# First units of GLU, up and embed in another order: two first contraction halves, then both second halves

## Chip, core and metric

The kernel runs on one core of a Trainium2 chip. The metric is the device time of one execution in microseconds (us), lower being better. Three runs of the kernel before took 1865.04, 1866.92 and 1867.5 us; their median is 1866.92 us.

## What is computed

Two layers over a sequence of 512 positions of 1024 channels, each with a mixer, a gated feed-forward part with a small convolution, and a per-layer embedding. The mixer of layer 0 is a bidirectional SSD, that of layer 1 an S5 state model whose output goes through a GLU.

```
h = x
for i in range(2):
    u = rmsnorm(h, mix_norm_w[i])
    h = h + (ssd_mixer if i == 0 else s5_mixer)(u, ...)
    h = h + conv_ffn(rmsnorm(h, ffn_norm_w[i]), w_up[i], conv_w[i], conv_b[i], w_down[i])
    h = h + (p[i] @ w_proj[i]) * sigmoid(rmsnorm(h, ple_norm_w[i]) @ w_gate[i])
return rmsnorm(h, final_norm_w)
# s5_mixer ends with:  g = gelu(y);  v = g @ w_glu + b_glu;  return v[:, :1024] * sigmoid(v[:, 1024:])
# rmsnorm(x, w) = x * rsqrt(mean(x * x) + 1e-6) * w
```

All is float32.

## The kernel before

**Layout and precision.** Everything stands transposed: 128 channels on the partitions, 512 positions in the free dimension, so `h` is 8 tiles of 128x512. Each large product is made of three fp32r products: the activation is split into a rounded part (`uh`, `gh`, `gh5`, `yh`) and a residual (`ul`, `gl`, `gl5`, `yl`), and so is the weight (`w_hi`, `w_lo`).

**Units.** Weights come in units of 128x1024: four contraction tiles by 256 output channels. SyncE loads a unit into one of two `w_raw` buffers, ScalarE rounds it to `w_hi` (`hi`, L848), VectorE subtracts to get `w_lo` (`lo`, L1193), and TensorE uses it in `product` (L1799 to L1801): 2 output tiles x 4 contraction tiles x 3 matmuls = 24 matmuls of 512 columns. There are two buffers of each kind. So the rounding of a unit waits until the unit two before it has been used (`unit_done`), and the load of a unit waits for the `w_lo` of the unit two before it. The contraction over 1024 channels takes two units (`kg` 0 and 1, the first and second contraction half), which add up in the same pair of PSUM tiles. Output tiles go round the four banks of `ring`.

**Order.** Each engine has one program, written out by hand, and works through it in order; semaphores join them. `hi_to(u)` and `lo_to(u)` round and subtract every unit up to u that isn't done yet. The place of such a call in an engine's program decides what the unit stands behind.

**The norm.** Gain and 1/rms are applied apart: `uh` and `ul` hold h times the gain, and the output tile is multiplied by `rstd` as it leaves PSUM. The sum of squares runs in parallel: ScalarE squares the tiles (L864), GpSimd adds up the first six, and TensorE sums over partitions with three matmuls with a matrix of ones into `pe_s` (`add_square`, L1810 and L1812; fp32). I call these three "the squares". Then VectorE makes mean plus epsilon (`rstd_of`, L1214), ScalarE the root (`std`, L872), VectorE the reciprocal (L1216). Until VectorE has passed this, nothing behind it in its program runs.

**The five starts.**
- *Up* (layers 0 and 1): units in the order (gate half, kg 0), (gate half, kg 1), (value half, kg 0), (value half, kg 1) for each pair of tiles, in a loop (`Fori`). VectorE takes two tiles with `rstd` (L1692), makes two convolution taps (L1702), products and residual; ScalarE the first tap and SiLU. In layer 0, ScalarE issues eight DMAs for S5 (L1100, L1104) and makes four copies `ptw` (L1113) between the root and the loop.
- *Down* is followed by *embed*: a projection unit (`proj_product`, L2135 to L2137, 12 matmuls), the squares, then eight gate units, two for each output pair, with a projection between the pairs. VectorE: `rstd_of`, `lo_to`, per pair two `cc` products (L1761), a `w_lo`, two products with the projection (L1767), the next `w_lo`, two additions to h (L1771). In layer 0 it also computes the tables of S5 (`tables`, L1521 to L1531) between these.
- *GLU*: S5 works in 8 blocks. For each, TensorE's output (L2049) is copied by ScalarE (`y_out`, L1042), goes to DRAM and back in another order, gets a skip term on VectorE (`skip`, L1623), GELU on ScalarE (`gelu`, L1048). Then ScalarE splits off `gh5` (`g5_split`, L1053) and VectorE `gl5` (`g5_rest`, L1629). All splits stand behind the loop over the blocks.

The lines that place embed's norm and first units on VectorE before:

```
u = U[("ple", layer)]
rstd_of(r)
lo_to(u + 2)
for i in range(4):
    lo_to(u + GATE[i] + 2)          # GATE = (1, 3, 6, 9)
    ...
    dve.wait_ge(unit_done, u + GATE[i] + 2)
    ... two cc products
    lo_to(u + GATE[i] + 3)
```

Of the kernel before, what the change touches and what calls it, by code (L numbers as in the profile page):

```python
# [90 lines left out]
def bidir_hybrid_kernel(nc, A, out):  # L91
    _, SEQ, D = A["x"].shape
    KD = D // P
# [37 lines left out]
    with ExitStack() as ctx:  # L131
# [258 lines left out]

        def unit_size(u):
# [28 lines left out]
        def _(sp):  # L420
# [156 lines left out]
            for layer, parts in enumerate(PARTS):  # L577
                wk = A["ffn_w_up"][layer].rearrange("(k p) n -> p k n", p=P)
                for part, (first, pairs) in enumerate(parts):
                    u = U[("up", layer, part)]  # L580
                    with sp.Fori(0, pairs) as i:
                        for half in range(2):
                            for kg in range(2):
                                load(u + 2 * half + kg,
                                     wk[:, 4 * kg:4 * kg + 4, bass.ds(i * 256 + (half * HID + first * 256), 256)],
                                     at=i * 4)
# [252 lines left out]
        def _(act):  # L839
# [167 lines left out]
            for layer, parts in enumerate(PARTS):  # L1007
                gh, gl, p_in, ph, pl = FFN[layer]
                if layer == 1:
# [56 lines left out]
                    for b in range(NB):  # L1066
# [26 lines left out]

                std(1 + 3 * layer)
# [91 lines left out]
        def _(dve):  # L1186
# [355 lines left out]
            for layer, parts in enumerate(PARTS):  # L1542
                gh, gl, p_in, ph, pl = FFN[layer]
                if layer == 1:
# [103 lines left out]
                    for b in range(NB):  # L1648
# [31 lines left out]

                rstd_of(1 + 3 * layer)
                r = 2 + 3 * layer
                for part, (first, pairs) in enumerate(parts):
# [3 lines left out]
                    with dve.Fori(0, pairs) as i:  # L1687
                        for half in range(2):
                            dve.wait_ge(unit_done, i * 4 + (u + 2 * half + 2))
# [4 lines left out]
                            lo(u + 2 * half + 3, at=i * 4)  # L1694
# [18 lines left out]
                        for j in range(2):  # L1713
# [3 lines left out]
                                              ALU.subtract).then_inc(f_gl, 1)  # L1717
                    split[0] = U[("down", layer, part)] + 2
# [28 lines left out]
                u = U[("ple", layer)]  # L1747
                rstd_of(r)
                lo_to(u + 2)
                before = 2 * KD * layer  # L1750
                for i in range(4):
# [3 lines left out]
                    dve.wait_ge(unit_done, u + GATE[i] + 2)  # L1755
# [31 lines left out]
        def _(pe):  # L1787
# [182 lines left out]
            for layer, parts in enumerate(PARTS):  # L1970
# [3 lines left out]
                if layer == 1:  # L1974
# [216 lines left out]
```

## Time and profile before

| | |
|---|---|
| median of 3 runs | 1866.92 us |
| the profiled execution | 1867.26 us |
| its span, first to last instruction | 1865.5 us |
| TensorE busy | 1635.2 us (88%) |
| VectorE busy | 1304.9 us (70%) |
| ScalarE busy | 718.4 us (39%) |
| GpSimd busy | 163.7 us (9%) |
| mean granted TensorE clock | 0.915 of full |

The profiled execution is one run; all durations below are from it. "Busy" says how long an engine worked, not whether anybody waited for it. Where TensorE stands still, the timeline names in brackets how long it had been idle and whose work released it. The release is inferred from semaphores.

### The profile page before, as it was taken

Reading aid. Unit: us, or ns where it says so; the run is one execution under the profiler, and the core shown is the slowest. Engines: PE = TensorE matmul, PEld = TensorE weight load, DVE = VectorE, ACT = ScalarE, POOL = GpSimd, SP = SyncE. Lnnn points to the kernel's source line nnn. Section 1 sums busy time; section 2 is a strip of 40 time slices with the busy share of each in tenths; the row PEclk is TensorE's granted clock in tenths of the full one; section 3 lists DMA queues with packets and bytes.
Section 4 is the critical chain, followed back from the end, with each engine's and each line's share of the span. In section 5 each row is a group of like instructions: output and inputs, shape, how many; then the busy total and the mean of one; then the engine's idle time right before and its main releaser. Section 6 shows DMA issues by size and latency. Waiting matters only on the chain.

```text
span 1865.5 us, 20894 instructions
## 1 busy us (share of the span) xinstructions
PE 1635.2 (88%) x7451; PEld 1298.1 (70%) x7451; DVE 1304.9 (70%) x1683; ACT 718.4 (39%) x1079; POOL 163.7 (9%) x200
## 2 busy tenths in 40 slices
PE   3986998998997879989998976878799999999996
PEld 1753766766765668878886755878686888888875
DVE  4587777776776667787769898999365776763355
ACT  3453452452452355532442332220234555542232
POOL 1151000000000180000001120000010000000100
PEclk7997998998998889999999986765799999999998
DMA  2320221211211342343343655652122223333231
GB/s 70 89 59 0 57 67 35 68 57 34 74 51 34 64 105 90 101 138 122 99 142 134 221 191 161 177 154 64 57 91 79 95 96 101 90 107 95 92 94 65
DMA packets 185174, 173.66 MB, mean 93 GB/s; under 512 B 47294, under 2 KB 177934, under 8 KB 181006
## 3 DMA queue, kind: packets, MB, share of 16 engines
q1 hardware_dynamic: 164494, 170.61, 29.4%
q10 hardware_dynamic: 20608, 2.10, 0.9%
q8 instruction: 44, 0.72, 0.2%
q14 instruction: 28, 0.23, 0.0%
HBM read 148.50 MB, written 24.18 MB: 93 GB/s over the span
## 4 chain that ended last, share of the span: by engine, by line
PE 65%; DVE 22%; issue 5%; ACT 4%; SPq 2%; DMA 1%; ACTq 1%; DVEq 0%
PE ring L1799 18%; PE ring L1800 18%; PE ring L1801 18%; DVE w_lo L1193 2%; PE pe_e L1870 2%; PE pe_e L1871 2%; PE pe_y L1948 1%; DVE rb L1601 1%; ACT rr L908 1%; DVE ul L1207 1%; PE ring L1932 1%; PE ring L1926 1%; PE pe_y L1943 1%; DVE cc L1312 1%; PE pe_s L2049 1%
## 5 line engine op out<-in xcount | busy, mean ns | idle before, releaser
L848 ACT ACTIVATE w_hi<-w_raw 128x1024 fp32r<-128x1024 f32 (+1 forms) x233 | 240.0, 1030 | 666.1 <-PE ring L1801 632.9
L1799 PE MATMUL ring<-uh,w_hi 128*128 128x512 f32 (+1 forms) x1160 | 461.3, 398 | 38.4 <-DVE w_lo L1193 32.0
L1800 PE MATMUL ring<-ul,w_hi 128*128 128x512 f32 (+1 forms) x1160 | 455.3, 393 | 0.0
L1801 PE MATMUL ring<-uh,w_lo 128*128 128x512 f32 (+1 forms) x1160 | 454.8, 392 | 0.0
L1193 DVE TENSOR_TENSOR w_lo<-w_raw,w_hi 128x1024 fp32r<-128x1024 f32 (+1 forms) x233 | 279.3, 1201 | 200.5 <-ACT w_hi L848 200.3
L1799 PEld LDWEIGHTS ring<-uh,w_hi 128*128 128x128 f32 (+1 forms) x1160 | 219.7, 189 | 96.7 <-DVE w_lo L1193 26.0
L1800 PEld LDWEIGHTS ring<-ul,w_hi 128*128 128x128 f32 (+1 forms) x1160 | 219.7, 189 | 47.3 <-issue 2.1
L1801 PEld LDWEIGHTS ring<-uh,w_lo 128*128 128x128 f32 (+1 forms) x1160 | 219.5, 189 | 47.1 <-issue 0.6
L1799 PE MATMUL ring<-gh,w_hi 128*128 128x512 f32 x480 | 190.8, 397 | 29.1 <-DVE w_lo L1193 16.0
L1800 PE MATMUL ring<-gl,w_hi 128*128 128x512 f32 x480 | 189.5, 395 | 0.0
L1801 PE MATMUL ring<-gh,w_lo 128*128 128x512 f32 x480 | 189.1, 394 | 0.0
L1692 DVE TENSOR_TENSOR cin<-ring,rstd 128x512 f32<-128x512 f32 x88 | 56.7, 687 | 113.9 <-PE ring L1801 113.9
L1799 PEld LDWEIGHTS ring<-gh,w_hi 128*128 128x128 f32 x480 | 91.7, 191 | 51.7 <-DVE w_lo L1193 19.0
L1702 DVE SCALAR_TENSOR_TENSOR cc<-cin,par,cc 128x512 f32<-128x512 f32 x176 | 123.5, 765 | 0.0
L1801 PEld LDWEIGHTS ring<-gh,w_lo 128*128 128x128 f32 x480 | 91.7, 191 | 19.6
L1800 PEld LDWEIGHTS ring<-gl,w_hi 128*128 128x128 f32 x480 | 91.8, 191 | 18.8
L660 POOL TENSOR_TENSOR var<-sq 128x512 f32<-128x512 f32 x7 | 9.8, 1399 | 796.2 <-ACT sq L864 728.9
L908 ACT ACTIVATE rr<-tri,ad_seq 128x128 f32<-128x128 f32 x256 | 76.4, 388 | 0.0
L1128 ACT ACTIVATE cc<-cin,par 128x512 f32<-128x512 f32 x88 | 66.9, 808 | 1.6 <-DVE cin L1692 1.5
L1312 DVE SCALAR_TENSOR_TENSOR cc<-cin,par,cc 128x512 f32<-128x512 f32 x96 | 65.2, 751 | 2.0 <-ACT cc L937 2.0
L1799 PE MATMUL ring<-yh,w_hi 128*128 128x512 f32 x128 | 55.0, 429 | 10.0 <-DVE yl L1482 10.0
L1207 DVE SCALAR_TENSOR_TENSOR ul<-h,par,uh 128x512 fp32r<-128x512 f32 x40 | 50.2, 1272 | 14.8 <-ACT uh L868 14.6
(249 smaller groups left out, 2206.0 us busy)
## 6 DMA issues: line engine op xcount, KB each, us to landing
w_raw<-in_ffn_w_up SPq DMA_DIRECT2D x88, 512.0 KB, 3.5
w_raw<-in_ffn_w_down SPq DMA_DIRECT2D x40, 512.0 KB, 3.5
w_raw<-in_ssd_w_in SPq DMA_DIRECT2D x32, 512.0 KB, 3.7
s_tables<-tab SPq DMA_DIRECT2D x16, 1024.0 KB, 6.1
slot<-s_tables SPq DMA_DIRECT2D x16, 1024.0 KB, 8.7
w_raw<-in_ssd_w_out SPq DMA_DIRECT2D x16, 512.0 KB, 3.5
w_raw<-in_ple_w_gate SPq DMA_DIRECT2D x16, 512.0 KB, 3.5
w_raw<-in_s_w_glu SPq DMA_DIRECT2D x16, 512.0 KB, 3.4
```

The lines of the kernel that those rows point to most:

```text
L848: act.activation(w_hi[u % 2][:, 0:n], w_raw[:, u % 2, 0:n], ACT.Copy).then_inc(hi_done, 1)
L908: act.activation(rr[:, d, k, c, :], m[:], ACT.Copy, scale=ad_seq[:, c, at:at + 1]).then_inc(r_done, 1)
L1128: act.activation(cc[:, 2 * half + j, :], cin[:, j, 1:1 + SEQ], ACT.Identity, scale=dcol(i * 2 + (C_FCW + c)), bias=dcol(i * 2 + (C_FCB + 2 ...
L1193: dve.tensor_tensor(w_lo[u % 2][:, 0:n], w_raw[:, u % 2, 0:n], w_hi[u % 2][:, 0:n].bitcast(F32), ALU.subtract).then_inc(lo_done, 1)
L1207: dve.scalar_tensor_tensor(out=ul[:, m, :], in0=h[:, m, :], scalar=col(NORM_COL[r] + m), in1=uh[:, m, :].bitcast(F32), op0=ALU.mult, op1=A ...
L1312: dve.scalar_tensor_tensor(out=cc[:, q % 4, :], in0=cin[:, j, tap:tap + SEQ], scalar=col(C_CONVW + tap * CONV_T + chans[j]), in1=cc[:, q % ...
L1692: dve.tensor_tensor(cin[:, j, 2:2 + SEQ], bank(t + 2 * half + j), rstd[:], ALU.mult).then_inc(evac, 1)
L1702: dve.scalar_tensor_tensor(out=cc[:, 2 * half + j, :], in0=cin[:, j, 1 + tap:1 + tap + SEQ], scalar=dcol(i * 2 + (C_FCW + c)), in1=cc[:, 2 ...
L1799: pe.matmul(o, wh[:, k, c], rh[:, k0 + k, :], start=first and k == 0, stop=False)
L1800: pe.matmul(o, wh[:, k, c], rl[:, k0 + k, :], start=False, stop=False)
L1801: mm_ = pe.matmul(o, wl[:, k, c], rh[:, k0 + k, :], start=False, stop=last and k == nk - 1)
L1870: pe.matmul(pe_e[:, k, :], gt[:], rr[:, 0, k].rearrange("p c l -> p (c l)"), start=True, stop=False)
```

## The change

At five starts, the first four units come in the order (pair 0, kg 0), (pair 1, kg 0), (pair 0, kg 1), (pair 1, kg 1); the table of this order is `FIRST`, that of before `IN_TURN`. For up and GLU the two "pairs" are the first two halves of the output, for embed the first two pairs of output tiles. The weight loads follow the same order. TensorE's squares move from ahead of the first unit to behind the second one (up and embed). ScalarE rounds up's third unit ahead of the root, VectorE subtracts up's and embed's third unit ahead of `rstd_of`. The first pass of up's loop is written out on SyncE, TensorE and VectorE. In S5, six of the eight splits move: on ScalarE four go into block 6 and two into block 7, ahead of `y_out`; on VectorE six go ahead of the last `skip`.

```diff
+        FIRST = ((0, 0), (1, 0), (0, 1), (1, 1))
+        IN_TURN = ((0, 0), (0, 1), (1, 0), (1, 1))
...
@@ ScalarE, S5 and up
+                        if b >= NB - 2:
+                            act.wait_ge(y5_full, NB - 3)
+                            for m in range(4 * (b - NB + 2), 2 * b - 8):
+                                g5_split(m)
                         y_out(b)
-                    for m in range(NB - 2):
-                        g5_split(m)
                     gelu(NB - 1)
...
+                hi_to(U[("up", layer, 0)] + 2)
                 std(1 + 3 * layer)
@@ VectorE
+                    dve.wait_ge(y5_full, NB - 2)
+                    for m in range(KD - 2):
+                        g5_rest(m)
                     skip(NB - 1)
-                    for m in range(KD):
+                    for m in range(KD - 2, KD):
                         g5_rest(m)
...
-                            lo_to(u + 4 * i + 2 * half + 2)
-                            dve.wait_ge(unit_done, u + 4 * i + 2 * half + 2)
+                            lo_to(u + 4 * i + 2 * half + (2 if i or half else 3))
+                            dve.wait_ge(unit_done, u + 4 * i + 2 * half + (2 if i or half else 3))
...
+                lo_to(U[("up", layer, 0)] + 2)
                 rstd_of(1 + 3 * layer)
...
+                    def up_tiles(i, peeled=False):
                         for half in range(2):
+                            mixed = peeled and half == 0
+                            if mixed:
+                                lo(u + 3)
+                            dve.wait_ge(unit_done, i * 4 + (u + 2 * half + (3 if mixed else 2)))
...
                 u = U[("ple", layer)]
+                lo_to(u + 2)
                 rstd_of(r)
-                lo_to(u + 2)
...
-                    dve.wait_ge(unit_done, u + GATE[i] + 2)
+                    dve.wait_ge(unit_done, u + GATE[i] + (2 if i else 3))
@@ TensorE
-                add_square(r, KD - 2)
-                add_square(r, KD - 1)
...
+                    if part == 0:
+                        for n, (half, kg) in enumerate(FIRST):
+                            pe.wait_ge(ul_done, KD * SPLIT[r] + 4 * kg + 4)
+                            product(u + n, t + 2 * half, 4, 4 * kg, uh, ulo, first=kg == 0, last=kg == 1)
+                            if n == 1:
+                                add_square(r, KD - 2)
+                                add_square(r, KD - 1)
...
-                add_square(r + 1, KD - 2)
-                add_square(r + 1, KD - 1)
-                pe.wait_ge(ul_done, KD * SPLIT[r + 1] + KD)
                 for i in range(4):
                     for kg in range(2):
-                        product(u + GATE[i] + kg, T[("gate", layer, i // 2)] + i % 2 * 2, 4, 4 * kg, uh, ulo,
-                                first=kg == 0, last=kg == 1)
+                        col_, kk = FIRST[2 * i + kg] if i < 2 else (i, kg)
+                        if i < 2:
+                            pe.wait_ge(ul_done, KD * SPLIT[r + 1] + 4 * kk + 4)
+                        product(u + GATE[i] + kg, T[("gate", layer, col_ // 2)] + col_ % 2 * 2, 4, 4 * kk, uh, ulo,
+                                first=kk == 0, last=kk == 1)
+                        if (i, kg) == (0, 1):
+                            add_square(r + 1, KD - 2)
+                            add_square(r + 1, KD - 1)
```

**VectorE, start of embed in layer 1.** Before, from the last `w_lo` and the last two `ul` on:

```order
L1193 TENSOR_TENSOR w_lo<-w_raw,w_hi 128x1024
L1207 SCALAR_TENSOR_TENSOR ul<-h,par,uh 128x512 x2
L1214 TENSOR_SCALAR var<-pe_s 128x512
L1216 RECIPROCAL rstd<-var 128x512
L1193 TENSOR_TENSOR w_lo<-w_raw,w_hi 128x1024 x2
L1761 TENSOR_TENSOR cc<-ring,rstd 128x512 x2
L1193 TENSOR_TENSOR w_lo<-w_raw,w_hi 128x1024
L1767 TENSOR_TENSOR cc<-cc,pe_e 128x512 x2
```

The same engine and place now (L1205 is `lo`, L1219 `u_lo`, L1226 and L1228 `rstd_of`, L1787 and L1793 the products):

```order
L1205 TENSOR_TENSOR w_lo<-w_raw,w_hi 128x1024
L1219 SCALAR_TENSOR_TENSOR ul<-h,par,uh 128x512 x2
L1205 TENSOR_TENSOR w_lo<-w_raw,w_hi 128x1024
L1226 TENSOR_SCALAR var<-pe_s 128x512
L1228 RECIPROCAL rstd<-var 128x512
L1205 TENSOR_TENSOR w_lo<-w_raw,w_hi 128x1024
L1787 TENSOR_TENSOR cc<-ring,rstd 128x512 x2
L1205 TENSOR_TENSOR w_lo<-w_raw,w_hi 128x1024
L1793 TENSOR_TENSOR cc<-cc,pe_e 128x512 x2
```

One of the two `w_lo` behind the reciprocal has moved ahead of the mean; the other is still behind the reciprocal, and a third behind the `cc` products.

**TensorE, the same place.** Before, from the end of the first projection on (buffer numbers 0 and 1 tell units apart):

```order
L2135 MATMUL pe_e<-ph1,w_hi1 128x512
L2136 MATMUL pe_e<-pl1,w_hi1 128x512
L2137 MATMUL pe_e<-ph1,w_lo1 128x512
L1810 MATMUL pe_s<-var,ones 128x512
L1812 MATMUL pe_s<-sq,ones 128x512 x2
L1799 MATMUL ring<-uh1,w_hi0 128x512
L1800 MATMUL ring<-ul1,w_hi0 128x512
L1801 MATMUL ring<-uh1,w_lo0 128x512
```

Now, where the second gate unit ends and the third begins:

```order
L1825 MATMUL ring<-uh1,w_hi1 128x512
L1826 MATMUL ring<-ul1,w_hi1 128x512
L1827 MATMUL ring<-uh1,w_lo1 128x512
L1836 MATMUL pe_s<-var,ones 128x512
L1838 MATMUL pe_s<-sq,ones 128x512 x2
L1825 MATMUL ring<-uh1,w_hi0 128x512
L1826 MATMUL ring<-ul1,w_hi0 128x512
L1827 MATMUL ring<-uh1,w_lo0 128x512
```

The squares stood between the projection and the first gate unit, and stand between the second and the third.

**ScalarE, start of up in layer 0.** Before, from the last `uh` to the loop (L872 is the root, L1113 the `ptw` copies):

```order
L868 ACTIVATE uh<-h,par 128x512
L872 ACTIVATE var<-var 128x512
L1100 DMA tab<-in_s_b_re 64x64x16 x2
L1100 DMA tab<-in_s_b_im 64x64x16 x2
L1104 DMA tab<-in_s_c_re 128x8x64 x2
L1104 DMA tab<-in_s_c_im 128x8x64 x2
L1113 ACTIVATE ptw<-v 64x8x64 x4
L848 ACTIVATE w_hi<-w_raw 128x1024
L1120 UNCONDITIONAL_BRANCH
```

And now (L857 is `hi`, L881 the root):

```order
L877 ACTIVATE uh<-h,par 128x512
L857 ACTIVATE w_hi<-w_raw 128x1024
L881 ACTIVATE var<-var 128x512
L1112 DMA tab<-in_s_b_re 64x64x16 x2
L1112 DMA tab<-in_s_b_im 64x64x16 x2
L1116 DMA tab<-in_s_c_re 128x8x64 x2
L1116 DMA tab<-in_s_c_im 128x8x64 x2
L1125 ACTIVATE ptw<-v 64x8x64 x4
L1132 UNCONDITIONAL_BRANCH
```

The rounding of up's third unit has gone from behind the DMAs and copies to ahead of the root; the fourth unit's is in the loop, behind all of them, as before.

## Rows read from the trace of the kernel before

**Rows 1.** List of waits, TensorE: total us, times, longest.

```profile
PE ring L1799 <- DVE w_lo L1193: 48.0, 20, 12.4
```

**Rows 2.** Timeline, ScalarE, GLU: start us, us, instruction, idle before.

```profile
1346.66 1.06 ACT L848 ACTIVATE w_hi<-w_raw 128x1024 fp32r<-128x1024 f32 x1 [4.38 <-PE ring L1801]
```

**Rows 3.** Timeline, TensorE, embed of layer 1.

```profile
1785.73 1.02 PE L1810 MATMUL pe_s<-var,ones 128*128 128x512 f32 x2
...
1794.57 0.50 PE L1799 MATMUL ring<-uh,w_hi 128*128 128x512 f32 x1 [0.63 <-DVE w_lo L1193]
...
1811.04 0.39 PE L2135 MATMUL pe_e<-ph,w_hi 128*128 128x512 f32 x1
```

**Rows 4.** Timeline, ScalarE, embed of layer 1.

```profile
1794.03 1.06 ACT L848 ACTIVATE w_hi<-w_raw 128x1024 fp32r<-128x1024 f32 x1 [4.17 <-PE ring L1801]
```

**Rows 5.** Timeline, VectorE, embed of layer 1.

```profile
1788.51 0.69 DVE L1214 TENSOR_SCALAR var<-pe_s 128x512 f32<-128x512 f32 x1 [1.12 <-PE pe_s L1812]
1789.90 3.35 DVE L1216 RECIPROCAL rstd<-var 128x512 f32<-128x512 f32 x1 [0.70 <-ACT var L872]
1793.29 1.22 DVE L1193 TENSOR_TENSOR w_lo<-w_raw,w_hi 128x1024 fp32r<-128x1024 f32 x1
...
1800.36 1.29 DVE L1761 TENSOR_TENSOR cc<-ring,rstd 128x512 f32<-128x512 f32 x2 [4.01 <-PE ring L1801]
```

**Rows 6.** Timeline, TensorE, embed of layer 0, third output pair.

```profile
1079.77 0.80 PE L1799 MATMUL ring<-uh,w_hi 128*128 128x512 f32 x1 [6.18 <-DVE w_lo L1193]
...
1085.06 0.43 PE L1799 MATMUL ring<-uh,w_hi 128*128 128x512 f32 x1
```

**Rows 7.** Timeline, VectorE, embed of layer 0.

```profile
1044.73 1.22 DVE L1193 TENSOR_TENSOR w_lo<-w_raw,w_hi 128x1024 fp32r<-128x1024 f32 x1
...
1077.31 1.28 DVE L1761 TENSOR_TENSOR cc<-ring,rstd 128x512 f32<-128x512 f32 x2
```

**Rows 8.** Stretch, VectorE: us, busy (count), TensorE clock, DMA share, GB/s.

```profile
1060.04:1077.31 17.27, 14.84 (x16) 1.00 0.34 125
```

**Rows 9.** Timeline, TensorE, start of up in layer 0.

```profile
637.19 1.13 PE L1810 MATMUL pe_s<-var,ones 128*128 128x512 f32 x2 [0.21 <-POOL var L664]
...
664.52 0.79 PE L1799 MATMUL ring<-uh,w_hi 128*128 128x512 f32 x1 [12.36 <-DVE w_lo L1193]
```

**Rows 10.** Timeline, ScalarE, start of up in layer 0.

```profile
642.11 0.63 ACT L872 ACTIVATE var<-var 128x512 f32<-128x512 f32 x1 [1.42 <-DVE var L1214]
...
662.67 1.06 ACT L848 ACTIVATE w_hi<-w_raw 128x1024 fp32r<-128x1024 f32 x1
...
677.69 1.06 ACT L848 ACTIVATE w_hi<-w_raw 128x1024 fp32r<-128x1024 f32 x1 [1.91 <-PE ring L1801]
```

**Rows 11.** Timeline, VectorE, up in layer 0.

```profile
667.19 5.74 DVE L1702 SCALAR_TENSOR_TENSOR cc<-cin,par,cc 128x512 f32<-128x512 f32 x4
673.34 1.69 DVE L1193 TENSOR_TENSOR w_lo<-w_raw,w_hi 128x1024 fp32r<-128x1024 f32 x1 [0.41 <-ACT w_hi L848]
```

**Rows 12.** Costliest groups (page, part 5): busy us, mean ns, idle before.

```profile
L1702 DVE SCALAR_TENSOR_TENSOR cc<-cin,par,cc 128x512 f32<-128x512 f32 x176 | 123.5, 765 | 0.0
```

**Rows 13.** Timeline, TensorE, start of the GLU.

```profile
1321.98 0.76 PE L1799 MATMUL ring<-gh,w_hi 128*128 128x512 f32 x1 [11.73 <-issue]
```

**Rows 14.** Timeline, VectorE, end of S5.

```profile
1318.72 0.75 DVE L1623 SCALAR_TENSOR_TENSOR cin<-u,par,cin 128x512 f32<-128x512 f32 x1 [13.35 <-DMA cin<-s_y]
1319.39 4.90 DVE L1629 TENSOR_TENSOR gl<-u,gh 128x512 fp32r<-128x512 f32 x8
```

**Rows 15.** Timeline, ScalarE, end of S5.

```profile
1320.04 1.13 ACT L1053 ACTIVATE gh<-u 128x512 fp32r<-128x512 f32 x2
```

**Rows 16.** Timeline, TensorE, start of up in layer 1.

```profile
1417.38 3.78 PE L1812 MATMUL pe_s<-sq,ones 128*128 128x512 f32 x4 [4.63 <-ACT sq L864]
```

**Rows 17.** Timeline, ScalarE, up in layer 1.

```profile
1443.95 1.06 ACT L848 ACTIVATE w_hi<-w_raw 128x1024 fp32r<-128x1024 f32 x1 [1.92 <-PE ring L1801]
```

**Rows 18.** Stretch: us, busy of TensorE, its loads, VectorE, ScalarE, GpSimd; clock, DMA.

```profile
642.11:656.15 14.04, 10.05 (x45) 7.99 (x43) 3.35 (x1) 0.63 (x1) 1.10 (x1) 0.96 0.99 132
```

More of the change, by code:

```diff
@@ L491, in glu_load @@
             def glu_load(n):
-                i, half, kg = n // 4, n // 2 % 2, n % 2
+                i = n // 4
+                half, kg = (IN_TURN if i else FIRST)[n % 4]
                 load(U["glu"] + n, rows(A["s5_w_glu"][0], 4 * kg, 4, half * D + 256 * i, 256))
@@ L580, in _, with up_loads @@
                     u = U[("up", layer, part)]
[L581 to L586, printed above, removed]
+                    def up_loads(i, order):
+                        for n, (half, kg) in enumerate(order):
+                            load(u + n, wk[:, 4 * kg:4 * kg + 4, bass.ds(i * 256 + (half * HID + first * 256), 256)],
+                                 at=i * 4)
+                    if part == 0:
+                        up_loads(0, FIRST)
+                    with sp.Fori(int(part == 0), pairs) as i:
+                        up_loads(i, IN_TURN)
                     if part == len(parts) - 1:
@@ L613, in _ @@
                     for kg in range(2):
-                        load(u + GATE[i] + kg, rows(A["ple_w_gate"][layer], 4 * kg, 4, 256 * i, 256))
+                        half, kk = FIRST[2 * i + kg] if i < 2 else (i, kg)
+                        load(u + GATE[i] + kg, rows(A["ple_w_gate"][layer], 4 * kk, 4, 256 * half, 256))
                         if kg == 1 and i:
@@ L1693, in _ @@
                                                   ).then_inc(evac, 1)
-                            lo(u + 2 * half + 3, at=i * 4)
+                            if not mixed:
+                                lo(u + 2 * half + 3, at=i * 4)
                             for tap in range(1, 3):
@@ L1717, in _ @@
                                               ALU.subtract).then_inc(f_gl, 1)
+                    if part == 0:
+                        up_tiles(0, True)
+                    with dve.Fori(int(part == 0), pairs) as i:
+                        up_tiles(i)
                     split[0] = U[("down", layer, part)] + 2
@@ L2071, in _ @@
                     for i in range(4):
-                        for half in range(2):
-                            for kg in range(2):
-                                if i == 0 and half == 0:
-                                    pe.wait_ge(g5_lo, 4 * kg + 4)
-                                product(u + 4 * i + 2 * half + kg, t + 4 * i + 2 * half, 4, 4 * kg, gh5, gl5,
-                                        first=kg == 0, last=kg == 1)
+                        for n, (half, kg) in enumerate(IN_TURN if i else FIRST):
+                            if i == 0:
+                                pe.wait_ge(g5_lo, 4 * kg + 4)
+                            product(u + 4 * i + n, t + 4 * i + 2 * half, 4, 4 * kg, gh5, gl5, first=kg == 0, last=kg == 1)
                         if i:
@@ L2080, in _ @@
                             add_square(4, 2 * i - 1)
[L2081 to L2082 removed]
                 for part, (first, pairs) in enumerate(parts):
                     u, t = U[("up", layer, part)], T[("up", layer, part)]
[L2086 to L2092 removed]
+                    if part == 0:
+                        for n, (half, kg) in enumerate(FIRST):
[4 more added lines that the diff above has]
+                                add_square(r, KD - 1)
+                    with pe.Fori(int(part == 0), pairs) as i:
+                        for n, (half, kg) in enumerate(IN_TURN):
+                            product(u + n, t + 2 * half, 4, 4 * kg, uh, ulo, at=i * 4, first=kg == 0, last=kg == 1)
                     if (layer, part) == (0, 0):
```

10 lines of the change are left out of this document (removed).

## Prediction

> **What bounds the kernel now.** I read the page first: TensorE is busy for 88% of the span, so only what makes it wait, or run slowly, counts. Next the list of waits on TensorE: the largest entry is its wait for w_lo, the residual of a weight unit that VectorE writes, 48.0 us in 20 waits [rows 1]. Then, in each place that the change touches, the timelines of TensorE, VectorE and ScalarE side by side. The price of a unit (24 matmuls) comes from the GLU: ScalarE idles 4.38 us, rounds for 1.06 us, and so meets a unit every 5.44 us. A rounding that waits for TensorE starts 0.25 us after the unit's last issue [rows 2]; I take unit ends from such rows.
>
> The change swaps units at five starts: GLU, up in both layers, embed in both layers. u0 to u3 are the first four units there. Before, u0 and u1 finish one output pair; now u0 and u1 are the first halves of two pairs, and u2 and u3 the second halves. The matmuls are the same. What moves is the three ones-matmuls of the norm (the squares): from ahead of u0 to behind u1, at up and embed. Everything below is what now waits for them.
>
> **Embed, layer 1.** Before: the squares start at 1785.73 [rows 3], u0 ends at 1794.03 - 0.25 = 1793.78 [rows 4], so the squares cost 8.05 - 5.44 = 2.6. A wait of 0.63 for w_lo of u1, then u1 to u3 run through to the projection at 1811.04 [rows 3]. After: u0 and u1 take 1785.7 to 1796.6; the squares end at 1799.2. u2 needs its w_lo, and the new VectorE order puts only one w_lo ahead of the mean, the other behind the reciprocal. From the end of the squares: 0.2 until the mean (1788.51), 1.39 to the reciprocal, 3.39 to the w_lo, 1.28 to the matmul [rows 3, 5] = 6.26. TensorE stands from 1799.2 to 1805.5. Before, the same 6 us lay beside u0. After an idle of 6.18 in layer 0, the twelve matmuls from 1079.77 to 1085.06 took 5.29 instead of 2.72 [rows 6], which is 1.2 in place of 2.4 GHz: 2.6 more. u2 ends at 1813.5. Then w_lo of u3 stands on VectorE behind the two cc products that need u2: 0.24 + 1.29 [rows 5] + 1.28 = 2.8, which was hidden under u2 before. u3 runs from 1816.3 to 1821.7 against 1811.04: **+10.7**. The end of the kernel follows this chain. Bounds: 8.1 if the clock doesn't fall; 13.3 if the pause of 2.8 costs another 2.6.
>
> The Trainium skill (TensorE: Matmul & The Clock Gate, "What's actually happening") calls the number of slow matmuls variable from one run of a kernel to the next. The trace agrees so far as its own slow phases differ (2.6 here, 2.0 at up in layer 0, below). By the row the term is 10.7; by the rule with the smaller phase it is 10.1.
>
> **Embed, layer 0.** The same, with VectorE also making the S5 tables. The last w_lo ahead of u0 starts at 1044.73 [rows 7], so u0 can start at 1046.0; u1 ends at 1056.9, the squares at 1059.5, u2 starts at 1065.8 and ends at 1073.8, its cc products start at 1074.05. From there VectorE is the bound: from one pair's cc (1060.04) to the next (1077.31) 17.27 passed, 14.84 of it busy [rows 8]; the rest was waiting for a load and for ScalarE that are now early. So the next cc is at 1074.05 + 14.84 = 1088.9, and the fifth unit 2.46 later, as before (1079.77 - 1077.31, [rows 6, 7]), at 1091.35: **+11.6**. TensorE idles in front of it as before, so its clock is no worse. Bounds: 9.0 without the slow phase; 14.0 if the old waits of 2.4 stay. The S5 phase starts from this chain and moves with it.
>
> **Up, layer 0.** Before: the squares could start at 637.19 - 0.21 = 637.0 [rows 9]; u2 waited 12.36 for w_lo [rows 9], because ScalarE, behind the square root at 642.11, issued eight DMAs and made four ptw copies before the next rounding; u3 ended at 677.69 - 0.25 = 677.4 [rows 10]. Now the rounding of u2 goes ahead of the root, so u2 doesn't wait. But the squares go behind u1: 637.0 + 10.9 + 2.6 = 650.5, the root at 651.3, 9.2 later, with DMAs and copies behind it. The rounding of u3 was at 662.67 [rows 10], less one rounding that has gone: 662.67 - 1.06 + 9.2 = 670.8. Its w_lo starts at 671.9, takes 1.7 with GpSimd active beside it [rows 11], and u3 starts at 673.7. TensorE has stood since 650.5 + 5.4 = 655.9, for 17.8 in place of 12.4. With a slow phase of 2.0 (664.52 to 677.4 was 12.9 for two units) u3 ends at 681.1. The next w_lo stands behind four taps: start 675.2, 5.74 for the four, 1.69 for w_lo [rows 11], matmul at 682.7. So **+5.3**. Bounds: 2 if the taps take half of that and the DMAs gain 1.6 by not meeting a weight load; 8 if GpSimd's products slow the w_lo to 2.9.
>
> In [rows 11] four taps took 5.74, while the mean of one over the kernel is 0.765 [rows 12]. The Trainium skill (SBUF — State Buffer, "Who interferes with whom") says that a VectorE instruction with two SBUF inputs contends with a GpSimd instruction that reads SBUF; the taps have two. GpSimd moves with the DMAs, so by this rule the overlap stays and the term is 5.3; with no overlap it would be 3.7.
>
> **GLU.** TensorE was free at 1321.98 - 11.73 = 1310.25 [rows 13]. It waited for VectorE's gl5, eight in a row from 1319.39 for 4.90, behind a skip at 1318.72 that waited 13.35 for a DMA [rows 14]. Six of the eight move into that idle time, from 1318.72 - 13.35 = 1305.4 on: six by 0.61 end at 1309, and u0 and u1 need only the first four. Their ScalarE halves move into idle time too, ahead of the stage's last two copies. The clock was low before 1321.98 and after: u0 to u3 took 24.43 up to 1346.41 (1346.66 - 0.25, [rows 2]) in place of 21.76, so 2.67 for the slow phase. After: u0 1310.25 to 1318.4, u1 to 1323.8. ScalarE's last split ends at 1320.04 + 1.13 [rows 15]; rounding and w_lo of u2 are ready at 1321.17 + 1.06 + 1.28 = 1323.5, just in time. u3 ends at 1334.7: **-11.7**. Bounds: -12.0 (the w_lo is then the limit) and -9.2 if all of u0 is at 1.2 GHz (24 x 0.44 = 10.6 for 8.1).
>
> **Up, layer 1.** The squares' second matmul at 1417.38 had waited 4.63 for the last pair [rows 16]; their first, of 1.02 as in [rows 3], began at 1411.73, where TensorE was free. A slow phase followed; u3 ended at 1443.95 - 0.25 = 1443.7 [rows 17]. After: u0 and u1 1411.7 to 1422.6, squares to 1425.2, u2 to 1430.7, and w_lo of u3 is ready 6.26 after the squares, 1431.5. u3 ends at 1436.9: **-6.8**. Bounds: -7.6 and -5.5 (a second wait of 1.3 behind the taps).
>
> **Sum.** 10.7 + 11.6 + 5.3 - 11.7 - 6.8 = +9.1. The profiled execution took 1867.26 (span 1865.5), 0.34 above the median shown: 1867.26 + 9.1 - 0.34 = **1876.0 us**. The first pass of the up loop is now written out; I cost that at nothing, since the GLU's written-out units also follow each other at 5.44 [rows 2]. So are the swapped weight loads: each goes at the same point of SP's queue, with the same bytes from another address.
>
> **Rivals.**
> A, faster: the eight DMAs of layer 0. DMA engines were 99% busy during their issue [rows 18]. If ScalarE is held only because a weight load stands in the same engines, the 14.0 us from the root (642.11) to the copies (656.15) shrink to about 2; u3 of up starts 12.0 earlier, its taps no longer delay the fifth unit by 1.6, and the sum is 9.1 - 12.0 - 1.6 = -4.5, 1862.4. It decides if the issue shrinks by more than 9. Against it: one weight load is under way there, and the eight move four times its bytes, half of them in pieces of 64 B by the code.
> B, no change: no slow phase after the two embed pauses, nor contention in layer 0: 8.1 + 9.0 + 2 - 12 - 6.8 = +0.3, 1867.2. For it: after a pause of 0.63 only the first matmul was longer (0.50, [rows 3]). Against: pauses of 4.63 and 6.18 were followed by matmuls of 0.63 or twice the usual spacing.
> C, slower still: a second slow phase at embed in layer 1 (13.3), GLU's first unit all at 1.2 GHz (-9.2), old waits kept in layer 0 (14.0): 13.3 + 14.0 + 8 - 9.2 - 5.5 = +20.6, 1887.5. It needs every bound at once; half of that way, about +15, is what I give a chance.
> D, the change doesn't do what it says: GLU's splits don't come forward, because of the new waits for y5_full; then 11.7 is lost and the sum is +20.8, 1887.7. Both waits are for output stages two or more before the last, so this is unlikely.
>
> **Chances.** Forecast within its bounds 0.74, A 0.07, B 0.10, C 0.07, D 0.02. A change under 0.2% (3.7 us) can't be told from none: faster is A, 0.07; the same is B and the low edge of the forecast, 0.13; slower is the rest, 0.80. Range 1868.5 to 1882.5: it holds the forecast with its bounds partly adding up, and half of B.
>
> **What would show it.** In the profile after: a TensorE wait for w_lo of about 6 us in each embed between the squares and the next unit, followed by 0.63 us matmuls; a second one of nearly 3 in layer 1; a wait of about 18 in layer 0's up; the GLU's first matmul at once behind the last S5 output; no wait at layer 1's squares. If the embed waits are missing, the forecast is wrong at its root.

## The result, and the profile after

The changed kernel takes 1874.88 us (median of 5 runs, 1874.78 to 1878.62), the kernel before 1866.57 us beside it (5 runs, 1864.35 to 1867.5). The ratio is 1.0052, 95% interval 1.0037 to 1.0066: slower by 7 to 12 us. 1876.0 had been forecast.

The list of waits on TensorE (total us, times, longest) answers to [rows 1]:

```profile
PE ring L1825 <- DVE w_lo L1205: 70.9, 25, 17.6
```

22.9 us more of waiting for `w_lo`, in five more waits. The wait of 11.73 in the GLU [rows 13] has gone. TensorE is still busy for 87%; the change shows in the waits and in the clock behind them.

**Embed, layer 1.** TensorE's timeline (start, us, instruction, idle before and what released it), for [rows 3]:

```profile
1780.87 0.47 PE L1825 MATMUL ring<-uh,w_hi 128*128 128x512 f32 x1
...
1791.84 1.02 PE L1836 MATMUL pe_s<-var,ones 128*128 128x512 f32 x2
...
1800.76 0.77 PE L1825 MATMUL ring<-uh,w_hi 128*128 128x512 f32 x1 [6.18 <-DVE w_lo L1205]
...
1803.88 0.59 PE L1826 MATMUL ring<-ul,w_hi 128*128 128x512 f32 x1
...
1810.75 0.47 PE L1825 MATMUL ring<-uh,w_hi 128*128 128x512 f32 x1 [2.60 <-DVE w_lo L1205]
...
1814.40 0.47 PE L1825 MATMUL ring<-uh,w_hi 128*128 128x512 f32 x1
...
1817.92 0.39 PE L2160 MATMUL pe_e<-ph,w_hi 128*128 128x512 f32 x1
```

VectorE beside it, for [rows 5]:

```profile
1794.61 0.69 DVE L1226 TENSOR_SCALAR var<-pe_s 128x512 f32<-128x512 f32 x1 [10.67 <-PE pe_s L1838]
1796.00 3.35 DVE L1228 RECIPROCAL rstd<-var 128x512 f32<-128x512 f32 x1 [0.70 <-ACT var L881]
1799.39 1.23 DVE L1205 TENSOR_TENSOR w_lo<-w_raw,w_hi 128x1024 fp32r<-128x1024 f32 x1
1808.18 1.29 DVE L1787 TENSOR_TENSOR cc<-ring,rstd 128x512 f32<-128x512 f32 x2 [7.57 <-PE ring L1827]
1809.39 1.22 DVE L1205 TENSOR_TENSOR w_lo<-w_raw,w_hi 128x1024 fp32r<-128x1024 f32 x1
```

Mean at 1794.61, reciprocal, `w_lo` at 1799.39, u2 at 1800.76: the chain that used to lie beside u0 now has TensorE standing in front of it. The second wait is the `w_lo` of u3 behind the two `cc` products. From u0 (1780.87) to the next projection (1817.92) pass 37.05 us; before it was 1811.04 - 1785.73 = 25.31 [rows 3]. The term is +11.7.

Stretches of the same place (start and end, us, TensorE busy and its matmuls, granted clock, DMA share, GB/s):

```profile
1785.00:1791.00 6.00, 6.00 (x28) 1.00 0.27 87
1794.60:1800.70 6.10, 0.00 (x0) 0.74 0.00 0
1800.80:1803.90 3.10, 3.10 (x8) 0.50 0.26 85
1804.50:1808.00 3.50, 3.50 (x16) 1.00 0.00 0
1808.20:1810.70 2.50, 0.00 (x0) 1.00 0.00 0
1811.10:1814.40 3.30, 3.30 (x10) 0.50 0.65 187
```

Behind each of the two pauses the granted clock is 0.50 for a while: 1.2 in place of 2.4 GHz, 0.43 us a matmul in place of 0.23. I call this a slow phase. Each of the two costs about 1.7: the 24 matmuls of u2 take 7.2 from their first start, those of u3 as well, in place of 5.44.

**Embed, layer 0.** TensorE, for [rows 6]; the last line is the third output pair's:

```profile
1045.87 0.47 PE L2160 MATMUL pe_e<-ph,w_hi 128*128 128x512 f32 x1 [1.20 <-DVE w_lo L1205]
...
1070.33 0.77 PE L1825 MATMUL ring<-uh,w_hi 128*128 128x512 f32 x1 [6.18 <-DVE w_lo L1205]
...
1080.29 0.47 PE L1825 MATMUL ring<-uh,w_hi 128*128 128x512 f32 x1 [2.61 <-DVE w_lo L1205]
...
1094.83 0.80 PE L1825 MATMUL ring<-uh,w_hi 128*128 128x512 f32 x1 [4.49 <-DVE w_lo L1205]
```

The projection before, where the term starts:

```profile
1041.50 0.47 PE L2135 MATMUL pe_e<-ph,w_hi 128*128 128x512 f32 x1 [1.17 <-DVE w_lo L1193]
```

From the projection to the third pair: 48.96, against 38.27 before (1041.50 to 1079.77). The term is +10.7. Here too each of the two pauses has a slow phase behind it.

**Up, layer 0.** TensorE, ScalarE and VectorE, for [rows 9 to 11]:

```profile
672.48 0.77 PE L1825 MATMUL ring<-uh,w_hi 128*128 128x512 f32 x1 [17.59 <-DVE w_lo L1205]
...
681.15 0.49 PE L1825 MATMUL ring<-uh,w_hi 128*128 128x512 f32 x1 [0.40 <-DVE w_lo L1205]
```

```profile
650.19 0.63 ACT L881 ACTIVATE var<-var 128x512 f32<-128x512 f32 x1 [7.62 <-DVE var L1226]
650.19 3.29 ACTq L1112 DMA_DIRECT2D tab<-in_s_b_re  x2
653.51 5.39 ACTq L1112 DMA_DIRECT2D tab<-in_s_b_im  x2
658.94 3.21 ACTq L1116 DMA_DIRECT2D tab<-in_s_c_re  x2
662.18 2.19 ACTq L1116 DMA_DIRECT2D tab<-in_s_c_im  x2
664.42 4.12 ACT L1125 ACTIVATE ptw<-v 64x512 f32<-64x512 f32 x4 [13.61 <-issue]
```

```profile
674.05 4.86 DVE L1723 SCALAR_TENSOR_TENSOR cc<-cin,par,cc 128x512 f32<-128x512 f32 x4 [0.52 <-ACT cc L1140]
678.84 2.18 DVE L1205 TENSOR_TENSOR w_lo<-w_raw,w_hi 128x1024 fp32r<-128x1024 f32 x1
```

The eight DMAs hold ScalarE for 14.2 us again, now behind a root 8 us later. u4 starts at 681.15, 3.7 later than before (677.4); this run came to the place 1.0 earlier, so the term is +4.7.

**GLU and up, layer 1.** TensorE, for [rows 13 and 16]:

```profile
1323.21 0.77 PE L1825 MATMUL ring<-gh,w_hi 128*128 128x512 f32 x1
...
1337.05 0.47 PE L1825 MATMUL ring<-gh,w_hi 128*128 128x512 f32 x1 [1.17 <-DVE w_lo L1205]
...
1424.21 1.02 PE L1836 MATMUL pe_s<-var,ones 128*128 128x512 f32 x2
...
1433.13 0.47 PE L1825 MATMUL ring<-uh,w_hi 128*128 128x512 f32 x1 [0.72 <-DVE w_lo L1205]
```

The GLU's first matmul follows the last S5 output at once. From the end of that output (1323.45, 0.24 behind the first matmul's start) u0 to u3 take 24.6, where 36.16 had passed before (1310.25 to 1346.41): -11.5. The squares of up no longer wait 4.63. From the end of the GLU's u3 to the start of embed in layer 1 it takes 6.5 less than before; that is up's term, -6.5.

The S5 phase in between, from VectorE's first instruction (the fill of `erot`) to TensorE's last output, took 187.8 before and 185.9 after. It starts 15.1 later than before, just as the third pair of embed does. Most of its blocks take 20.2; one is longer where VectorE's skip product waits for its data from DRAM. Such a wait before and after:

```profile
1255.42 0.75 DVE L1623 SCALAR_TENSOR_TENSOR cin<-u,par,cin 128x512 f32<-128x512 f32 x1 [1.69 <-DMA cin<-s_y]
...
1248.91 0.75 DVE L1635 SCALAR_TENSOR_TENSOR cin<-u,par,cin 128x512 f32<-128x512 f32 x1 [0.66 <-DMA cin<-s_y]
```

Over the fourteen profiled kernels of this study the phase took 184.8 to 188.8. It isn't free of a tie to the edits: the seven kernels with embed in layer 0 as before have 187.3 in the mean and such a longer block each, the seven with the new order there 185.6, and five of them have none. The latter all start S5 later, and nothing here separates the order from the later start. So whether the 1.9 us are scatter or given back by the change stays open.

The sum: 4.7 + 10.7 - 11.5 - 6.5 + 11.7 - 1.9 = +7.2, and -1.0 for the earlier arrival makes +6.2; the spans differ by 7.6. The other 1.4 lie in two places with the same work in both kernels. Between u4 of up and embed in layer 0 the delay grows by 0.7, with slow phases of other lengths on the way: behind a pause of 5.99 in down, 11 slow matmuls before and 7 after, behind one of 6.37 there, 8 before and 14 after. And the last transposes of the kernel take 6.24 in place of 5.10; from their start to the end of the span it is 0.7 more.

### The profile page after: what moved, and what is told of

It reads as the page before. It is cut to its first block, busy times and chain, and to the rows that moved or that the text cites. A ratio compares the mean times of both kernels' runs of the same rounds, so it can differ in the third digit from the quotient of the medians.

```text
span 1873.1 us, 20795 instructions
## 1 busy us (share of the span) xinstructions
PE 1637.9 (87%) x7451; PEld 1301.5 (69%) x7451; DVE 1306.2 (70%) x1683; ACT 717.5 (38%) x1079; POOL 163.7 (9%) x200
## 4 chain that ended last, share of the span: by engine, by line
PE 67%; DVE 22%; ACT 4%; issue 4%; DMA 1%; SPq 1%; ACTq 1%; DVEq 0%
PE ring L1825 19%; PE ring L1826 18%; PE ring L1827 18%; DVE w_lo L1205 2%; PE pe_e L1896 2%; PE pe_e L1897 2%; DVE rb L1613 2%; PE pe_y L1974 1%; ACT rr L917 1%; PE ring L1958 1%; DVE rstd L1228 1%; PE ring L1952 1%; PE pe_y L1969 1%; DVE cc L1324 1%; DVE ul L1219 1%
## 5 line engine op out<-in xcount | busy, mean ns | idle before, releaser
L857 ACT ACTIVATE w_hi<-w_raw 128x1024 fp32r<-128x1024 f32 (+1 forms) x233 | 239.6, 1029 | 613.9 <-PE ring L1827 584.4
L1205 DVE TENSOR_TENSOR w_lo<-w_raw,w_hi 128x1024 fp32r<-128x1024 f32 (+1 forms) x233 | 278.3, 1196 | 184.6 <-ACT w_hi L857 184.3
L1827 PE MATMUL ring<-gh,w_lo 128*128 128x512 f32 x480 | 188.8, 393 | 0.0
L2075 PE MATMUL pe_s<-xs,slot 128*128 128x64 f32 x256 | 49.9, 385 | 16.4 <-DVE xs L1626 16.4
```

The costliest lines, as they stand in the source:

```text
L857: act.activation(w_hi[u % 2][:, 0:n], w_raw[:, u % 2, 0:n], ACT.Copy).then_inc(hi_done, 1)
L1205: dve.tensor_tensor(w_lo[u % 2][:, 0:n], w_raw[:, u % 2, 0:n], w_hi[u % 2][:, 0:n].bitcast(F32), ALU.subtract).then_inc(lo_done, 1)
L1827: mm_ = pe.matmul(o, wl[:, k, c], rh[:, k0 + k, :], start=False, stop=last and k == nk - 1)
L2075: mm_ = pe.matmul(pe_s[:, NCH * g:NCH * g + NCH], slots[b % 4][:, 1, at:at + P], xs[:, a, g, :], start=False, stop=a == 1, skip_group_chec ...
```

## Experiments

All were timed beside the kernel before, whose median was 1865.6, 1865.3, 1866.5 and 1865.4 in the four groups of runs.

**The embed part undone.** Loads, order on TensorE and order on VectorE as before; all else as changed.

```diff
+                add_square(r + 1, KD - 2)          # TensorE, ahead of the gate units
+                add_square(r + 1, KD - 1)
...
-                lo_to(u + 2)                       # VectorE
                 rstd_of(r)
+                lo_to(u + 2)
```

> The kernel after with the embed part alone as before (order of units, squares ahead of u0, VectorE's order); GLU and up keep the change. Theory (the two embed starts cost 10.7 and 11.7, as the profile after shows): 1874.9 - 22.4 = 1852.5 us. Rival (the S5 phase takes a later start back, 1.9 in the profile after, and would do so less from an earlier one): 1854.4. Rival (the cost sits elsewhere, in the loop's first pass written out or in the swapped loads of up): above 1865.

Measured: 1851.71 us, ratio 0.9924 (0.9907 to 0.9940). From 1.0052 that is 24 us: the embed starts cost more than the whole loss, and the other three places together gain 14.

**Squares ahead again, the new order kept.** VectorE's mean and reciprocal go back ahead of the `w_lo` with them, which the cut edit doesn't show.

```diff
                 proj_product(0)
+                add_square(r + 1, KD - 2)
+                add_square(r + 1, KD - 1)
...
-                        if (i, kg) == (0, 1):
-                            add_square(r + 1, KD - 2)
-                            add_square(r + 1, KD - 1)
```

> The kernel after with embed's squares back ahead of u0 and VectorE's mean and reciprocal ahead of that w_lo, as before; the new order of the four units and its loads stay. Theory (the cost is the chain squares, mean, root, reciprocal, w_lo laid bare): the waits of about 6.2 us in both layers go, the slow phases behind them too. What stays is the wait for u3's w_lo behind the cc products (2.6, in layer 1 with a slow phase of 1.7) and a later first cc in layer 0: about 4.3 + 4 over embed as before, so 1861 us. Rival (the interleaved order and its loads cost the 22 us): about 1875, no change. Rival (the squares are all of it): 1852.5.

Measured: 1858.77 us, ratio 0.9958 (0.9941 to 0.9975). Of the 23 us between the kernel after and the one with embed undone, 16 go with the place of the squares and 7 stay with the new order. What stays in layer 1 is one pause, for the `w_lo` of u3 behind the `cc` products, and a slow phase with it:

```profile
1795.76 0.76 PE L1825 MATMUL ring<-uh,w_hi 128*128 128x512 f32 x1 [2.61 <-DVE w_lo L1205]
```

**Squares behind u1, but both `w_lo` ahead of mean and root.**

```diff
-                hi_to(u + 2)                       # ScalarE
+                hi_to(u + 4)
                 std(r)
...
-                lo_to(u + 2)                       # VectorE
+                lo_to(u + 4)
                 rstd_of(r)
```

> The kernel after with the squares still behind u1 at embed, but the roundings and w_lo of u2 and u3 ahead of the root (ScalarE) and of the mean (VectorE). Theory (only the place of w_lo behind the reciprocal costs, not the place of the squares): both waits go. Layer 1: u0 to u3 and the squares take 24.4 from 1785.7, 0.9 less than before the change; layer 0: the first cc comes at u2's end, 5.4 later than before, and VectorE works 14.8 to the next, so 2.7 more. 1852.5 - 0.9 + 2.7 = 1854 us. Rival (squares behind u1 delay the normalised output whatever the order of w_lo, and the wait comes back at the cc products): 1862 or more.

Measured: 1858.16 us, ratio 0.9956 (0.9939 to 0.9973). Right in layer 1, where no wait is left. In layer 0 the waits for u2 and u3 are gone too, but not the delay. VectorE and ScalarE there:

```profile
1065.60 1.23 DVE L1205 TENSOR_TENSOR w_lo<-w_raw,w_hi 128x1024 fp32r<-128x1024 f32 x1 [7.41 <-ACT w_hi L857]
1066.75 0.68 DVE L1226 TENSOR_SCALAR var<-pe_s 128x512 f32<-128x512 f32 x1
```

```profile
1064.51 1.06 ACT L857 ACTIVATE w_hi<-w_raw 128x1024 fp32r<-128x1024 f32 x1 [7.58 <-DMA w_raw<-in_ple_w_gate]
```

In layer 0 u3's weights land only at 1064.5: SyncE issued their load at 1052.9, right behind three transfers of S5 tables. Whether these held it up, no run shows. The mean was queued behind the `w_lo` of u3: it starts 5.7 behind the start of the squares, 2.8 in the kernel after. That is 2.9 of the 7.4 us that the place has over before. Behind the mean stand root, reciprocal and three table products, and the first `cc` comes right behind them at 1074.93, though u2 was done long before. So the expected 2.7 left out two things: a wait that I hadn't looked for, and that the squares' place delays the first `cc` by itself, as the rival said.

**Only u3's `w_lo` moved ahead of the `cc` products.**

```diff
-                    lo_to(u + GATE[i] + 2)
+                    lo_to(u + GATE[i] + (2 if i else 3))
```

> The kernel after with one edit at embed: VectorE makes w_lo of u3 ahead of the first two cc products. The wait of 6.2 for u2 stays. Theory 1 (the second wait of 2.60 in layer 1 brings the second slow phase of 1.7): both go, and in layer 0, where VectorE is the bound, little: -4.3, 1870.6 us, and no 0.56 us matmuls in u3 of layer 1. Theory 2 (the second slow phase would come without a second wait, as a late part of the first): only the 2.6 goes, 1872.3, and slow matmuls remain in u3.

Measured: 1869.81 us, ratio 1.0020 (1.0011 to 1.0030). In layer 1 the pause of 2.60 is gone, and with it the second slow phase; the first ran longer. Stretches of this kernel, columns as above:

```profile
1800.10:1804.80 4.70, 4.70 (x11) 0.50 0.53 167
1805.30:1813.00 7.70, 7.70 (x36) 1.00 0.03 6
```

The four, measured in the two places against before (layer 0: projection to third pair; layer 1: u0 or squares to the next projection):

| kernel | layer 0, us | layer 1, us | sum over before |
|---|---|---|---|
| before | 38.27 | 25.31 | |
| embed undone | 38.23 | 25.33 | 0.0 |
| squares ahead | 41.06 | 29.61 | +7.1 |
| both `w_lo` ahead | 45.64 | 24.47 | +6.5 |
| u3's `w_lo` ahead | 48.10 | 33.26 | +17.8 |
| after | 48.96 | 37.05 | +22.4 |

Added to 1851.7, the sums give 1858.8, 1858.2, 1869.5 and 1874.1; measured were 1858.8, 1858.2, 1869.8 and 1874.9. The two places carry the difference to within 0.8; as the S5 phase alone varies by more, so close a match is partly luck.

**The GLU's splits alone**, on the kernel before.

```diff
                             gelu(b - 1)
+                        if b >= NB - 2:
+                            act.wait_ge(y5_full, NB - 3)
+                            for m in range(4 * (b - NB + 2), 2 * b - 8):
+                                g5_split(m)
                         y_out(b)
-                    for m in range(NB - 2):
-                        g5_split(m)
...                                                # VectorE's g5_rest alike
```

> The kernel before with one part of the GLU's change: ScalarE's and VectorE's splits made inside the S5 loop, the GLU's units still in their old order, embed and up as before. Theory (the split move frees u0, the order frees u1): u0 starts at once at 1310.3, but u1 is now a second contraction half and stands until the last two splits are there, 1322.4 (13.1 earlier than 1335.5 in the profile after), and a slow phase of 2.3 follows: u3 ends at 1322.5 + 16.3 + 2.3 = 1341.1 in place of 1346.4: -5.3 against the kernel before. Rival (the split move is all of the gain): -11.5. Rival (u1 waits for the last splits anyway, so nothing without the order): 0.

Measured: 1859.16 us, ratio 0.9969 (0.9957 to 0.9982). u1 is now what waits:

```profile
1307.85 0.77 PE L1804 MATMUL ring<-gh,w_hi 128*128 128x512 f32 x1
...
1320.00 0.80 PE L1804 MATMUL ring<-gh,w_hi 128*128 128x512 f32 x1 [4.51 <-DVE gl L1631]
```

**Splits and order of the GLU**, on the kernel before.

```diff
-                        for half in range(2):
-                            for kg in range(2):
-                                if i == 0 and half == 0:
-                                    pe.wait_ge(g5_lo, 4 * kg + 4)
...
+                        for n, (half, kg) in enumerate(IN_TURN if i else FIRST):
+                            if i == 0:
+                                pe.wait_ge(g5_lo, 4 * kg + 4)
...
```

> The kernel before with the GLU's part of the change alone, splits and order of units. Theory (terms add up): -11.5 against the kernel before, 1855 us, and 5 to 7 us under the kernel with the splits alone. Rival (part of what the profile after shows in the GLU comes from the S5 phase having started later, and is not there without it): -9.6.

Measured: 1854.63 us, ratio 0.9942 (0.9925 to 0.9958). From TensorE's being free to the end of u3 it takes 24.7 us, 31.3 with the splits alone, 36.2 before. So by the rows the split move is worth 4.9 and the order 6.6; the medians give 6.1 and 4.5, with an S5 phase 0.8 longer in the second kernel.

**Up in layer 0 undone.** The rounding and `w_lo` of u2 go back behind the root as well.

```diff
-                        up_loads(0, FIRST)
+                        up_loads(0, FIRST if layer else IN_TURN)
...
+                        if layer == 0:             # TensorE, ahead of the units
+                            add_square(r, KD - 2)
+                            add_square(r, KD - 1)
```

> The kernel after with up in layer 0 alone back in the old order (squares ahead of u0, units in turn, rounding and w_lo of u2 behind the root), the loop's first pass still written out. Theory (the later squares make the wait for u3 longer, 17.6 against 12.4): 1874.9 - 4.7 = 1870.2 us, the longest wait for w_lo back at 12.4. Rival (the write-out of the first pass costs part of it): between 1870.2 and 1874.9 in the measure that it does. Rival (the start of the next phase swallows the term): 1874.9.

Measured: 1868.38 us, ratio 1.0020 (1.0011 to 1.0030), 6.5 under the kernel after by the medians, 5.0 by the profiled spans (1868.1 against 1873.1). From ScalarE's last rounding but one ahead of the place (632.15 here, 631.63 before, 630.63 after) to the projection of embed (1041.60, 1041.50 and 1045.87) pass 409.5, 409.9 and 415.2. The term is there, and the written-out pass shows no cost. But the wait of u2 is 10.32, not the expected 12.4: the written-out pass isn't the old start over again, and what shortened the wait is open.

**The DMAs ahead of the root, still on ScalarE.**

```diff
-                std(1 + 3 * layer)
                 if layer == 0:
...                                                # the eight DMAs
+                std(1 + 3 * layer)
```

> The kernel after with one edit: at up in layer 0 ScalarE issues its eight S5 DMAs ahead of the square root, in the 8.7 us in which it idles until the mean is there, in place of behind it. Theory (what holds u3 is ScalarE's queue: DMAs, ptw copies, then the rounding): the DMAs run from 642.5 to about 656.2, the copies end at 661, u3's w_lo is there at 663.8 in place of 672.4, so -8.6: 1866.3 us. Rival (the DMAs' own transfers or GpSimd beside them set the pace, so their place is of no use): 1872 or more. Rival (the DMAs now meet the weight load of u2 and u3 and take longer, 2 us each for eight): -5, 1870.

Measured: 1869.94 us, ratio 1.0027 (1.0016 to 1.0037), the last rival's 1870. ScalarE's queue:

```profile
642.11 3.38 ACTq L1111 DMA_DIRECT2D tab<-in_s_b_re  x2
645.52 8.29 ACTq L1111 DMA_DIRECT2D tab<-in_s_b_im  x2
```

The pair that lay over the weight load took 8.29 in place of 5.39; all eight took 16.7 in place of 14.2. u3 waits 11.93.

**The DMAs on SyncE's queue.** Two, three and three behind the loads of u1, u2 and u3.

```diff
+                            if s5 and n:           # SyncE, up_loads
+                                s5_in(n)
...
-                            act.dma_start(b_in[...], ...)
```

> The kernel after with one edit: the eight S5 DMAs of layer 0 are issued from SyncE's queue, two, three and three of them behind the weight loads of u1, u2 and u3 of up, in place of ScalarE's queue. Theory (ScalarE's hold of 14 us is what keeps u3's rounding back, not its place behind the squares as such): ScalarE has only the root and four ptw copies (4.1) ahead of it, u3's w_lo is there at 650.9 + 4.1 + 1.06 + 1.4 = 657.5 in place of 672.4, u3 waits about 3 us: -15 against the kernel after, 1860 us. Rival (the DMAs hold SyncE as long, and the weight loads behind them come late): half of it or less, 1867 or more, with w_hi waiting for DMA of w_raw. Rival (the squares' place is what costs): 1870 or more.

Measured: 1861.24 us, ratio 0.9978 (0.9967 to 0.9990), 13.6 under the kernel after. At the start of embed in layer 0 it is 12.0 ahead. ScalarE's hold was most of what kept u3 back: u3 now waits 5.35 in place of 17.59, and what keeps its rounding back is the four `ptw` copies and a table load:

```profile
651.13 4.36 ACT L1129 ACTIVATE ptw<-v 64x512 f32<-64x512 f32 x4
655.51 1.28 ACT L873 ACT_TABLE_LOAD   x1
656.80 1.06 ACT L873 ACTIVATE w_hi<-w_raw 128x1024 fp32r<-128x1024 f32 x1
```

**Combined: only what the runs had shown to gain.** GLU and up in layer 1 as changed, up and embed in layer 0 as before, embed in layer 1 with both `w_lo` ahead.

```diff
-                hi_to(u + 2)                       # embed; VectorE's lo_to alike
+                hi_to(u + (4 if layer else 2))
```

> What the runs point to, with nothing new in it: the GLU and up in layer 1 as changed; up and embed in layer 0 as before; embed in layer 1 in the new order with the roundings and w_lo of u2 and u3 ahead of root and mean. Theory (the terms add up): -11 - 6.5 - 0.9 = -18.4 against the kernel before, 1847 us. Rival (terms overlap, the S5 phase takes 2 of them back): 1849.

Measured: 1844.74 us, ratio 0.9884 (0.9868 to 0.9901), 2.3 below the forecast sum.

**Combined, DMAs on SyncE, u3's `w_lo` at up ahead of the mean.**

```diff
-                hi_to(U[("up", layer, 0)] + 2)     # VectorE's lo_to alike
+                hi_to(U[("up", layer, 0)] + 3)
```

> As the combined version (GLU and up in layer 1 as changed, embed in layer 0 as before, embed in layer 1 with w_lo ahead), but up in layer 0 in the new order with the rounding and w_lo of u3 ahead of root and mean, in both layers, and the eight S5 DMAs on SyncE's queue between the weight loads. Theory: at up in layer 0 TensorE stands nowhere: u0 to u3 and the squares end 24.4 after 637.0, at 661.4 in place of 677.4: -18.4 - 16 = -34, 1831 us. Rival (SyncE is held by the DMAs and u2's to u5's loads come late): 1840 or more.

Measured: 1841.53 us, ratio 0.9865 (0.9849 to 0.9882): the rival. u3's load, behind five DMAs, lands late, and the mean waits behind its `w_lo`:

```profile
655.38 1.06 ACT L873 ACTIVATE w_hi<-w_raw 128x1024 fp32r<-128x1024 f32 x1 [7.62 <-DMA w_raw<-in_ffn_w_up]
```

```profile
656.47 2.20 DVE L1215 TENSOR_TENSOR w_lo<-w_raw,w_hi 128x1024 fp32r<-128x1024 f32 x1 [7.45 <-ACT w_hi L873]
658.60 0.68 DVE L1236 TENSOR_SCALAR var<-pe_s 128x512 f32<-128x512 f32 x1
```

That is the mistake of embed in layer 0 once more. u4 then waits 5.95 for a `w_lo` behind the taps.

**The same without that last edit.** The first pass of up's loop, written out on ScalarE for it, goes back into the loop.

```diff
-                hi_to(U[("up", layer, 0)] + 3)     # VectorE's lo_to alike
+                hi_to(U[("up", layer, 0)] + 2)
```

> The kernel after with the S5 DMAs of layer 0 on SyncE's queue between the weight loads, embed in layer 0 as before and embed in layer 1 with w_lo of u2 and u3 ahead of root and mean; the rounding and w_lo of u3 at up in layer 0 stay behind the root. Theory (the terms add up; and ahead of the root, u3's rounding would only pass its wait for the late load on to the mean and the taps): 1861.2 for the DMAs on SyncE, less 23.9 (ratio 1.0052 for after, 0.9924 with embed undone, of 1866) and 0.9: 1836.5 us, 5 under the combined version with u3's w_lo ahead. Rival (VectorE's chain of taps sets the fifth unit in both): 1841.5, the same as that version.

Measured: 1836.28 us, ratio 0.9844 (0.9828 to 0.9860): 1.6% under the kernel before and 2.1% under the kernel after, the fastest version here. Of the 5.3 us under the version above, 5.2 are there at the start of embed in layer 0 (1032.56 against 1037.79), but 1.7 of these this run had already ahead of the place that the edit touches. So the edit is worth about 3.5. TensorE's waits for `w_lo`, for [rows 1]:

```profile
PE ring L1830 <- DVE w_lo L1209: 42.4, 22, 6.4
```

## Why the prediction was right

The mechanism came as forecast in all five places: each wait named beforehand is there, of about the forecast length. The five terms were off by +1.0, -0.9, -0.6, +0.2 and +0.3, which cancel to nothing, and the parts not forecast (-1.9, -1.0 and +1.4) nearly cancel too. That the time is longer, and by about this much, follows from the argument; that 1876.0 is within 1.2 us of the measured time is luck.

- **Embed, layer 1**: forecast +10.7, measured +11.7. Both pauses came at their size (6.26 and 2.8 forecast, 6.18 and 2.60 measured). The slow phase behind the first cost 1.7, not 2.6; the bound that the second pause would bring one of its own came true, at 1.7 as well. Undoing the part and moving the one `w_lo` show both.
- **Embed, layer 0**: forecast +11.6, measured +10.7. VectorE was the bound as argued, 14.63 from one `cc` to the next against 14.84 forecast. The slow phase in u2 was 1.8 and not 2.6, which is most of the 0.9 between them. A second pause and slow phase, in u3, weren't priced; as VectorE was the bound they hardly count (48.10 without them, 48.96 with them).
- **Up, layer 0**: forecast +5.3, measured +4.7, and 5.0 to 6.5 on undoing it. The wait of u3 was forecast at 17.8 and came at 17.6. The four taps took 4.86, less than before, the `w_lo` behind them 2.18, more.
- **GLU**: forecast -11.7, measured -11.5 and, alone, -10.6 by the medians. Two misses cancel here: u2 was to start just in time and waited 1.17, and the slow phase was 7 matmuls long, 12 before. **Up, layer 1**: -6.8 forecast, -6.5 measured.
- **Rivals.** A (the DMAs' issue shrinks) is refuted: 14.2 us again, and 16.7 where they met a weight load from the start. B (no slow phases) is refuted by the stretches at 0.50. D (no earlier splits) is refuted by the GLU's start. C's second slow phase in layer 1 came, but its other bounds didn't.
- **Not forecast**: the S5 phase, whose code no edit touches up to its last blocks, lasts 184.8 to 188.8 from one kernel to another. It took 1.9 off here, and why stays open.

## What to carry to other kernels

Putting a reduction later buys its own length only where something waited for its inputs; price what is queued behind its result on every engine (here mean, root and reciprocal: 4.8 us from the mean's start to the next `w_lo`). Moving such work ahead of the mean is the cure only if its own input is already there, or its wait is passed on to all that needs the mean. Small DMAs belong on a queue whose engine has slack: the same eight cost 13.6 us less from SyncE, though they held it as long as ScalarE.

## What the runs showed of the hardware

- The pause of 2.60 was followed by the lower clock too: in layer 1 the matmul after it began at full clock, and from 1811.1 to 1814.4 the granted clock was 0.50, with seven matmuls 0.43 us apart. Pauses of 6.18 were followed by 8 slow matmuls in the kernel after and 11 in the one with u3's `w_lo` ahead, and the pause of 6.37 in down, in code that is the same in both, by 8 before and 14 after. So the length of a slow phase isn't fixed by the pause. The Trainium skill (TensorE: Matmul & The Clock Gate, "What's actually happening") calls the number of slow matmuls variable from one run of a kernel to the next. Here the same code in two kernels differs in this way.
- ScalarE was held 14.2 us by the issue of eight DMAs of 256 KB, and 16.7 where a weight load was issued just ahead of the second pair; SyncE was held no less: from 636.4 to 654.8 with the weight loads between them.
